# Three groups of modulation columns, not four, over the four merge rounds of a fused transformer block

## The chip, the core and the metric

The kernel runs on one core of one Trainium2 chip. The metric is device microseconds of one execution. A core has a matrix engine (PE, with its weight loads shown as PEld), a vector engine (DVE), an activation engine (ACT), a general engine (POOL) and a queue engine (SP). Each works through its own instructions in order and waits on semaphores for the others. 16 DMA engines, shared by all queues, bring data in from memory.

## What is computed

Two transformer blocks on 256 tokens of width 2048, in float32. Most of the work is products of the 256 rows with weight matrices of 2048 rows and more. The second block is modulated: shifts, scales and gates come from one small product,

```
cond = silu(c)                       # 2048 values
mod  = cond @ mod_w + mod_b          # mod_w: 2048 x 12288
sh1, sc1, g1, sh2, sc2, g2 = split(mod, 6)
```

Nothing in the first block needs `mod`. The first block is: a mixer with three branches whose gated results are merged and projected (`w_o`), a cross attention, and a feed-forward (up 2048 to 2 x 4096 in two halves, a width-3 convolution, silu gate, down 4096 to 2048). The second block begins with the normalized, modulated input of its convolution mixer.

## The kernel before

**Weights.** Every weight matrix passes through SBUF in units of 512 KB (128 x 1024 values), four slots (`SLOTS`) in rotation. SP loads a unit into `raw`; ACT writes the rounded part `w_hi` (`round_units`, L613); DVE writes the rest `w_lo` (`rest_units`, L622); PE multiplies with both. A unit's `w_hi` can be written once PE is through with the unit four before it, and a unit's `raw` slot is free once its `w_lo` is written. A chunk is 512 result columns: eight units in most stages. The argument `k` of `rest_units` counts units from the start of a chunk; its range usually runs from 4 to 12, since DVE works ahead of PE.

**Modulation.** `mod` is computed beside the first block, in 8 groups of 1536 columns. A group is 16 units, one for each 128 rows of `mod_w`: POOL loads 128 x 1536 values into one of two buffers `mod_raw` (`load_mod`, L2195), DVE multiplies by a value of `cond` and adds into `mod_acc` (`mod_unit`, L1448; the first of a group, L1445, only multiplies). POOL's load number n waits for unit n - 2. After 16 units PE transposes `mod_acc` with 12 small matmuls (`mod_sum`, L1455) and DVE reduces and stores (`mod_keep`, L1463); the next group's first unit comes after that in DVE's order. The transposes go to banks 1 to 3 of `small`.

**The order on DVE is written by hand.** `rest_units(dve, s, first, last, between, times)` spreads `times` units over `last - first` weight units: after the n-th weight unit it makes those numbered from `n * times // of` to `(n + 1) * times // of`. Behind each weight chunk DVE also has the chunk's own work. The tables say how many units of modulation go where:

- the merge has 4 rounds; in each, chunks m = 0 to 2 (gates, 8 units each) and m = 3 to 5 (branches, 4, 2 and 2 units). One group per round: 5, 5, 4, 2, 0, 0 units. At the end of m = 3, 4, 5 DVE multiplies the sums by the gates (L2718), which frees the PSUM bank for the chunk two later
- `mix_out` (4 chunks): group 4, as 5, 5, 4, 2. `cross_q`: 6 units (`MOD_CROSS`)
- the feed-forward: for each half f four up pairs i (a chunk m = 0 and a chunk m = 1), `MOD_UP[f][i]` units in each, and four down chunks c with `MOD_DOWN[f][c]`. Where (f, i) is in `MOD_KEPT`, a group is summed and stored in chunk m = 0

In an up pair PE's matmuls go four banks at once (`multiply_two`, L701 and L703). Behind each up chunk DVE adds two halves of a result (`up_sum`, L2790), waits for ACT's newest tap, and makes two rows of taps (`up_tap`, L2808) between weight units; behind the pair it makes the product, its rounded part and its rest (L2852, L2855, L2857), the last of which tells PE that `y` is ready (`ff_split`). PE needs the fourth such `y` at the seventh unit of down chunk 0.

In the second half's down chunks DVE adds the sums to `h` (L2585), ACT squares them, DVE multiplies by `norm_final` (L2891, `nf_final`), and PE waits for that before the third unit of the next chunk (`down_before`, tile 4), where it transposes `h` (L935). In `down_ffn` the chunk c = 0 starts its own `rest_units` only at k = 7 (`LATE`), so its modulation units are spread over k = 7 to 10; the other chunks spread theirs over k = 4 to 10.

Of the kernel before, what the change touches and what calls it, by code (L numbers as in the profile page):

```python
# [26 lines left out]
KT = D // P  # L27
CH = 512
UK = 2
SLOTS = 4  # L30
# [161 lines left out]
def build_program(nc, x, mem, w_in, dn_conv, dn_a_log, dn_dt_bias, dn_norm, norm_mix, swa_sinks, w_br_dn, w_br_swa,  # L192
# [68 lines left out]
    with ExitStack() as ctx:  # L261
# [848 lines left out]

        def mem_norm_pe(pe):
            yield 10
            pe.wait_ge(mod_kept, 4)
            pe.wait_ge(norm_scaled, TT)
            for g in range(NG):
                turn_rows(pe, 1, mem_x, g, g + 1)
                yield 2
# [23 lines left out]
        def cross_norm_pe(pe):  # L1141
            yield 1
            pe.wait_ge(norm_gained, 2 * NG)
            mod_sum(pe, 5 * KT)
            yield 3
            pe.wait_ge(mod_kept, 5)
            pe.wait_ge(norm_scaled, 2 * TT)
            for g in range(0, NG, 2):
                turn_rows(pe, 2, norm_x2, g, g + 2)
                yield 1  # L1150
# [11 lines left out]
        def cross_norm_dve(dve, own):  # L1162
            rms_mean_dve(dve, 2)
            yield 1
            rms_rstd_dve(dve, own, 2)
            scale_rows(dve, h, norm_x2)
            yield 1
            mod_keep(dve, own, 4, 5)
            yield 1
            for g in range(0, NG, 2):  # L1170
                split_channels(dve, own, 2, norm_v2, y_hi, y_lo, g, g + 2)
                yield 1
# [892 lines left out]
        FF_STEPS = 4 * (FF_TAPS - 1)  # L2065
        LATE = 3
        MOD_CROSS = 6
        MOD_UP = (((0, 0), (3, 2), (2, 3), (0, 4)), ((2, 2), (0, 3), (2, 2), (2, 2)))
        MOD_KEPT = ((0, 3), (1, 1))
        MOD_DOWN = ((2, 2, 2, 2), (2, 2, 1, 0))  # L2070
        MERGE_L = (32, 6)
        w_in0, up0, down0, w1, w2 = w_in[0], w_up[0], w_down[0], mlp_w1_2[0], mlp_w2_2[0]

# [500 lines left out]
        def _(dve):  # L2574
# [120 lines left out]

            def merge(i, beside):
                L = (i, *MERGE_L)
                kt = 0

                def first_chunk(j):  # L2700
                    mod_unit(dve, j, j, (i, KT))
                    if j == 1 and not isinstance(i, int):
                        split_merged(bass.ds(i * 4 - 4, 4), at(0, (i, 1)))

                for m, units in enumerate((5, 5, 4, 2, 0, 0)):
                    s = spot("merge", m, L)
                    if m == 3 and beside is not None:
                        beside.rest()
                    end = s.size + SLOTS - (1 if m >= 3 else 0)
                    rest_units(dve, s, SLOTS, end,  # L2710
                               first_chunk if m == 0 else lambda j: mod_unit(dve, kt + j, kt + j, (i, KT)), units, beside)
                    kt += units
# [15 lines left out]
                    rest_units(dve, s, end, end + 1)  # L2728

            merge(0, beside)  # L2730
# [5 lines left out]
            for c, units in enumerate((5, 5, 4, 2)):  # L2736
                s = spot("mix_out", c % 2, (c // 2, 16, 2))

                def between(j):
                    mod_unit(dve, 4 * KT + kt + j, kt + j)  # L2740
# [14 lines left out]
            rest_units(dve, s, *ahead(s), lambda j: mod_unit(dve, 5 * KT + j, j), MOD_CROSS)  # L2755
            s = spot("mem_v", 0)
            beside = Beside(cross_soft_dve(dve, own))
            rest_units(dve, s, *ahead(s), beside=beside)
# [62 lines left out]
            for f in range(2):  # L2821
# [3 lines left out]
                for i in range(4):  # L2825
                    s = spot("ffn_up", 0, L, (i, 16, 2))
                    if (f, i) in MOD_KEPT:
                        rest_units(dve, s, SLOTS + LATE, s.size + 1)
                        mod_keep(dve, own, 5 + f, 6 + f)
# [233 lines left out]
        def _(pe):  # L3063
# [58 lines left out]
            def turn_merged(i):  # L3122

                pe.wait_ge(merge_sum, i + 1)
                pe.wait_ge(mod_kept, i + 1)
                for b in range(4):
                    for t in range(TT):
                        ins = pe.transpose(small[:, b // 2, (b % 2) * T + t * P:(b % 2) * T + (t + 1) * P],
# [10 lines left out]

                return before  # L3140

            def sum_before(i):

                def before(tile, end):
                    if tile == 2:
                        if i:
                            pe.wait_ge(merged, i)
                        mod_sum(pe, at(KT, (i, KT)))

                return before  # L3150

            def merge(i, beside):
                L = (i, *MERGE_L)
                for m in range(3):
                    multiply(pe, spot("merge", m, L), x_hi, x_lo, False,
                             before=merge_before(i - 1) if i and m == 0 else None, beside=beside)
                if beside is not None:
                    beside.rest()
                for m, k0 in ((3, 0), (4, 8), (5, 12)):
                    if i == 0:  # L3160
                        pe.wait_ge(y_split, m - 1)
                    multiply(pe, spot("merge", m, L), y_hi, y_lo, False, k0=k0, before=sum_before(i) if m == 5 else None)

            merge(0, beside)
            for i in range(1, 4):
# [44 lines left out]
            def half(f, first):  # L3210
                L = (f, FFN_U, FFN_C)
                for i in range(first, 4):
                    for m in range(2):
                        s = spot("ffn_up", m, L, (i, 16, 2))
                        if m and (f, i) in MOD_KEPT:
                            pe.wait_ge(mod_kept, 6 + f)
# [128 lines left out]
```

## Time and profile before

| | |
|---|---|
| median of 3 runs | 2616.12 us (2614.69 to 2625.41) |
| profiled execution | 2616.85 us, of which the profile's span is 2614.5 us |
| PE busy | 2552.7 us (98%) |
| PE weight loads busy | 2185.4 us (84%) |
| DVE busy | 1876.8 us (72%) |
| ACT busy | 1288.3 us (49%) |
| memory traffic | 553.14 MB, mean 212 GB/s, in 40 slices between 109 and 352 GB/s |
| mean granted clock of PE | 0.995 |

The page of the profile gives busy time by engine, the span in 40 slices, the chain of work that ended last and the costliest groups of instructions. PE's busy time is modelled (matmuls overlap), so a PE busy for 98% still has to be asked how far apart its matmuls start. On the chain that ended last PE has 79%, DVE 8%, DMA 7%, and of that the load of `mod_raw` 5%. In time, the merge rounds lie at about 420 to 790 us, `mix_out` and cross attention to 998 us, the feed-forward to 1545 us.

### The profile page before, as it was taken

To read this page: it belongs to the slowest core of one execution; us is meant where nothing else is said; L and a number is where in the kernel's file an instruction comes from. 1 tells how busy PE (TensorE), PEld (TensorE's weight loads), DVE (VectorE), ACT (ScalarE), POOL (GpSimd) and SP (SyncE) were. 2 spreads that over 40 slices of the span, in tenths; PEclk is the share of its full clock that TensorE was granted. 3 is DMA by queue.
4 is the path that set the end of the run, shared out by engine and by line. 5 is a ranking of instruction groups with operands and counts; after the bars stand their busy time and mean duration, and the time that the engine had idled before them with its cause. 6 is when DMAs were issued, how large, how long until landed. Compare 5 with 4: busy or idle time off the path is not lost.

```text
span 2614.5 us, 39013 instructions
## 1 busy us (share of the span) xinstructions
PE 2552.7 (98%) x14498; PEld 2185.4 (84%) x14498; DVE 1876.8 (72%) x2098; ACT 1288.3 (49%) x1681; POOL 235.5 (9%) x270
## 2 busy tenths in 40 slices
PE   8999999999999999999999999998999999999999
PEld 7888888877887888888888879996788888888887
DVE  6796658877888768887688757988566565565564
ACT  5645445543444446554455556676544344443443
POOL 2000000010010000000000005772000000000000
PEclk9999999999999999999999999998999999999999
DMA  6643437898999765778877744543555656666655
GB/s 210 173 133 109 136 114 268 298 319 302 320 352 326 257 220 173 249 269 283 262 242 258 245 154 147 160 153 113 177 171 189 194 178 195 183 192 193 192 186 168
DMA packets 291489, 553.14 MB, mean 212 GB/s; under 512 B 17121, under 2 KB 96018, under 8 KB 290578
## 3 DMA queue, kind: packets, MB, share of 16 engines
q1 hardware_dynamic: 270994, 442.06, 52.4%
q0 software_dynamic: 18720, 102.77, 11.7%
q10 hardware_dynamic: 1632, 6.29, 0.6%
q8 instruction: 103, 1.69, 0.3%
q14 instruction: 40, 0.33, 0.0%
HBM read 548.96 MB, written 2.10 MB: 211 GB/s over the span
## 4 chain that ended last, share of the span: by engine, by line
PE 79%; DVE 8%; DMA 7%; ACT 3%; issue 3%; SPq 0%; POOLq 0%; DVEq 0%; ACTq 0%
PE sums L668 30%; PE small L668 10%; PE small L701 9%; PE sums L701 9%; PE small L703 5%; DMA mod_raw<-in_mod_w_dram 5%; PE sums L703 4%; PE sums L720 4%; DVE w_lo L622 2%; PE sums L722 2%; DVE mod_acc L1448 2%; ACT w_hi L613 1%; PE small L1811 1%; DMA raw<-in_w_br_dn_dram 1%; PE sums L1948 0%
## 5 line engine op out<-in xcount | busy, mean ns | idle before, releaser
L613 ACT ACTIVATE w_hi<-raw 128x1024 fp32r<-128x1024 f32 x814 | 859.5, 1060 | 1179.3 <-PE sums L668 364.3
L622 DVE TENSOR_TENSOR w_lo<-raw,w_hi 128x1024 fp32r<-128x1024 f32 x814 | 1003.1, 1242 | 579.5 <-ACT w_hi L613 576.9
L701 PE MATMUL sums<-x_two,w_hi 128*128 128x512 f32 x1024 | 363.3, 399 | 4.0 <-DVE x_two L1046 2.3
L701 PE MATMUL small<-x_two,w_hi 128*128 128x512 f32 x1024 | 361.2, 397 | 0.0
L703 PE MATMUL sums<-x_two,w_lo 128*128 128x256 f32 x1024 | 288.0, 281 | 0.0
L703 PE MATMUL small<-x_two,w_lo 128*128 128x256 f32 x1024 | 287.4, 281 | 0.0
L668 PE MATMUL sums<-w_hi,x_two 128*128 128x512 f32 x896 | 281.7, 392 | 0.7 <-DVE w_lo L622 0.7
L668 PE MATMUL sums<-w_hi,y_hi 128*128 128x512 f32 x672 | 265.6, 395 | 13.6 <-issue 7.2
L668 PE MATMUL sums<-w_hi,y_lo 128*128 128x512 f32 x672 | 263.1, 392 | 0.0
L668 PE MATMUL sums<-w_lo,y_hi 128*128 128x512 f32 x672 | 263.0, 391 | 0.0
L1448 DVE SCALAR_TENSOR_TENSOR mod_acc<-mod_raw,cond,mod_acc 128x1536 f32<-128x1536 f32 x120 | 217.8, 1815 | 58.2 <-DMA mod_raw<-in_mod_w_dram 58.1
L701 PEld LDWEIGHTS sums<-x_two,w_hi 128*128 128x128 f32 x1024 | 193.0, 188 | 51.5 <-issue 5.0
L701 PEld LDWEIGHTS small<-x_two,w_hi 128*128 128x128 f32 x1024 | 192.2, 188 | 46.9
L720 PE MATMUL sums<-x_two,w_hi 128*128 128x512 f32 x608 | 221.4, 406 | 2.9 <-DVE w_lo L622 1.0
L668 PEld LDWEIGHTS sums<-w_hi,x_two 128*128 128x128 f32 x896 | 168.2, 188 | 36.8 <-DVE w_lo L622 1.1
L703 PEld LDWEIGHTS sums<-x_two,w_lo 128*128 128x128 f32 x1024 | 194.2, 190 | 0.2
L703 PEld LDWEIGHTS small<-x_two,w_lo 128*128 128x128 f32 x1024 | 193.4, 189 | 0.0
L668 PE MATMUL sums<-w_lo,x_two 128*128 128x512 f32 x448 | 174.4, 389 | 0.0
L722 PE MATMUL sums<-x_two,w_lo 128*128 128x256 f32 x608 | 170.4, 280 | 0.0
L668 PEld LDWEIGHTS sums<-w_hi,y_hi 128*128 128x128 f32 x672 | 127.2, 189 | 42.9 <-issue 9.2
L2195 POOL DMA_DIRECT2D mod_raw<-in_mod_w_dram x126 | 67.1, 532 | 1025.2 <-DVE mod_acc L1448 806.4
L1991 POOL TENSOR_TENSOR cv<-cv,cv_p 128x512 f32<-128x512 f32 x96 | 151.0, 1572 | 41.6 <-ACT cv_p L1975 29.6
(432 smaller groups left out, 3950.9 us busy)
## 6 DMA issues: line engine op xcount, KB each, us to landing
raw<-in_mlp_w_dram SPq DMA_DIRECT2D x256, 512.0 KB, 4.3
raw<-in_w_in_dram SPq DMA_DIRECT2D x198, 512.0 KB, 4.6
mod_raw<-in_mod_w_dram POOLq DMA_DIRECT2D x128, 768.0 KB, 6.5
raw<-in_w_up_dram SPq DMA_DIRECT2D x128, 512.0 KB, 4.4
raw<-in_w_down_dram SPq DMA_DIRECT2D x64, 512.0 KB, 4.6
raw<-in_conv_w_in_dram SPq DMA_DIRECT2D x128, 256.0 KB, 3.8
raw<-in_w_o_dram SPq DMA_DIRECT2D x32, 512.0 KB, 6.3
raw<-in_conv_w_out_dram SPq DMA_DIRECT2D x32, 512.0 KB, 4.0
```

Of the source, the lines that this page charges most:

```text
L613: act.activation(w_hi[:, s.slot(k), :], raw[:, s.slot(k), :], ACT.Copy).then_inc(hi_ready, 1)
L622: dve.tensor_tensor(w_lo[:, s.slot(k), :], raw[:, s.slot(k), :], w_hi[:, s.slot(k), :].bitcast(F32), ALU.subtract).then_inc(lo_ready, 1)
L668: mm = pe.matmul(o, l, r, start=first and i == 0, stop=end and i + 1 == len(steps), skip_group_check=True)
L701: pe.matmul(to[:, b, :], w_hi[:, s.slot(k), c], both, start=kt == 0, stop=False, skip_group_check=True)
L703: mm = pe.matmul(to[:, b, 0:T], w_lo[:, s.slot(k), c], x_two[:, kt, 0, :], start=False, stop=kt == KT - 1, skip_group_check=True)
L720: pe.matmul(sums[:, s.pair, b, :], w_hi[:, s.slot(k), c], both, start=kt == 0, stop=False, skip_group_check=True)
L722: mm = pe.matmul(sums[:, s.pair, b, 0:T], w_lo[:, s.slot(k), c], x_two[:, kt, 0, :], start=False, stop=kt == KT - 1, skip_group_check=True)
L1448: dve.scalar_tensor_tensor(out=mod_acc[:, :], in0=mod_raw[:, m % 2, :], scalar=c, in1=mod_acc[:, :], op0=ALU.mult, op1=ALU.add).then_inc(m ...
L1811: both = [pe.matmul(small[rows_of(d), bank + d, c], lhs[rows_of(d), c], rhs[rows_of(d), c], start=m == 0, stop=True, skip_group_check=True ...
L1991: ins = pool.tensor_tensor(o, o, cv_p[:, m % PRODUCTS, :, :], ALU.add)
L2195: pool.dma_start(mod_raw[:, slot, :], src).then_inc(mod_loaded[slot], 16)
```

## The change

The merge rounds take 12 units of modulation each, 48 in all, so three groups in place of four; a group now ends in round 1 at chunk 1, in round 2 at chunk 2 and in round 3 at chunk 5. Every later group moves one place on: `mix_out` makes group 3, `cross_q` begins group 4, and the feed-forward makes 58 units in place of 42, with three groups summed in up pairs and the last in the down chunks as before. The loads of POOL follow by themselves. DVE's loop over rounds 1 to 3 is written out.

```diff
         def mem_norm_pe(pe):
             yield 10
-            pe.wait_ge(mod_kept, 4)
+            pe.wait_ge(mod_kept, 3)
...
-            mod_sum(pe, 5 * KT)
+            mod_sum(pe, 4 * KT)
             yield 3
-            pe.wait_ge(mod_kept, 5)
+            pe.wait_ge(mod_kept, 4)
...
-            mod_keep(dve, own, 4, 5)
+            mod_keep(dve, own, 3, 4)
...
         MOD_CROSS = 6
-        MOD_UP = (((0, 0), (3, 2), (2, 3), (0, 4)), ((2, 2), (0, 3), (2, 2), (2, 2)))
-        MOD_KEPT = ((0, 3), (1, 1))
-        MOD_DOWN = ((2, 2, 2, 2), (2, 2, 1, 0))
+        MOD_MERGE = ((3, 3, 3, 2, 1, 0), (4, 0, 4, 2, 1, 1), (4, 4, 0, 2, 1, 1), (3, 3, 3, 2, 1, 0))
+        MOD_ENDS = ((1, 1), (2, 2), (3, 5))
+        MOD_UP = (((0, 0), (3, 2), (2, 3), (0, 4)), ((0, 4), (3, 3), (3, 3), (0, 4)))
+        MOD_KEPT = ((0, 3), (1, 0), (1, 3))
+        MOD_DOWN = ((3, 3, 3, 3), (4, 4, 4, 0))
...
-                for m, units in enumerate((5, 5, 4, 2, 0, 0)):
+                for m, units in enumerate(MOD_MERGE[i]):
...
                     if m < 3:
+                        if (i, m) in MOD_ENDS:
+                            q = MOD_ENDS.index((i, m))
+                            mod_keep(dve, own, q, q + 1)
                         continue
...
-                        mod_keep(dve, own, i, at(1, (i, 1)))
+                        if (i, m) in MOD_ENDS:
+                            mod_keep(dve, own, 2, 3)
...
-            with own.loop(4, 2, 1) as i:
+            for i in range(1, 4):
                 merge(i, None)
...
             def mods():
-                for m in range(5 * KT + MOD_CROSS, 8 * KT):
+                for m in range(4 * KT + MOD_CROSS, 8 * KT):
...
-                pe.wait_ge(mod_kept, i + 1)
+                if i:
+                    pe.wait_ge(mod_kept, i)
...
-            def sum_before(i):
+            def sum_before(i, m):
 
                 def before(tile, end):
-                    if tile == 2:
-                        if i:
-                            pe.wait_ge(merged, i)
-                        mod_sum(pe, at(KT, (i, KT)))
+                    if tile == (2 if m == 5 else 8):
+                        pe.wait_ge(merged, i)
+                        mod_sum(pe, KT * (MOD_ENDS.index((i, m)) + 1))
...
                     if tile == 8:
-                        added(pe, spot("ffn_up", 1, (f, FFN_U, FFN_C), (i - 1, 16, 2)))
-                        mod_sum(pe, (6 + f) * KT)
+                        if i:
+                            added(pe, spot("ffn_up", 1, (f, FFN_U, FFN_C), (i - 1, 16, 2)))
+                        else:
+                            added(pe, *(spot("ffn_down", m, (f - 1, FFN_U, FFN_C), (1, 16, 2)) for m in range(2)))
+                        mod_sum(pe, (5 + MOD_KEPT.index((f, i))) * KT)
```

## Rows read from the trace of the kernel before

**Rows 1.** Page, parts 5 and 6: ACT's rounding, and the modulation's loads (KB, us to landing).

```profile
L613 ACT ACTIVATE w_hi<-raw 128x1024 fp32r<-128x1024 f32 x814 | 859.5, 1060 | 1179.3 <-PE sums L668 364.3
...
mod_raw<-in_mod_w_dram POOLq DMA_DIRECT2D x128, 768.0 KB, 6.5
```

**Rows 2.** Windows: three merge rounds, then the second half's four up pairs (the columns are named).

```profile
core 0: us, PE busy (x) PEld busy (x) DVE busy (x) ACT busy (x) POOL busy (x), PEclk, DMA share, GB/s
509.35:605.62 96.27, 91.99 (x406) 74.90 (x405) 74.29 (x57) 37.64 (x36) 8.48 (x16) 0.98 0.90 306
605.62:696.85 91.23, 89.60 (x405) 74.08 (x404) 72.37 (x56) 37.55 (x36) 8.48 (x16) 1.00 0.92 319
696.85:786.85 90.00, 89.58 (x405) 74.09 (x404) 74.08 (x57) 37.54 (x36) 8.48 (x16) 1.00 0.92 327
1268.36:1450.56 182.20, 182.20 (x1038) 158.27 (x1036) 143.60 (x155) 89.37 (x103) 7.96 (x15) 1.00 0.76 247
```

**Rows 3.** Timeline, PE, merge: start us, us, engine, line, operation [idle before, releaser].

```profile
601.26 0.80 PE L668 MATMUL sums<-w_hi,y_hi 128*128 128x512 f32 x1 [2.69 <-DVE gate L2718]
...
605.62 1.47 PE L1455 MATMUL small<-ident,mod_acc 128*128 128x128 f32 x12
...
693.99 0.50 PE L668 MATMUL sums<-w_hi,y_hi 128*128 128x512 f32 x1 [1.63 <-DVE gate L2718]
...
784.00 0.50 PE L668 MATMUL sums<-w_hi,y_hi 128*128 128x512 f32 x1 [0.42 <-DVE gate L2718]
```

**Rows 4.** Timeline, DVE: first half of the feed-forward, second up pair, three units close together.

```profile
1056.41 1.22 DVE L2852 TENSOR_TENSOR ff_v<-ff_v,ff_g 128x1024 f32<-128x1024 f32 x1
...
1059.54 2.36 DVE L622 TENSOR_TENSOR w_lo<-raw,w_hi 128x1024 fp32r<-128x1024 f32 x2
1061.81 1.81 DVE L1448 SCALAR_TENSOR_TENSOR mod_acc<-mod_raw,cond,mod_acc 128x1536 f32<-128x1536 f32 x1
...
1064.67 1.81 DVE L1448 SCALAR_TENSOR_TENSOR mod_acc<-mod_raw,cond,mod_acc 128x1536 f32<-128x1536 f32 x1
...
1071.95 1.82 DVE L1448 SCALAR_TENSOR_TENSOR mod_acc<-mod_raw,cond,mod_acc 128x1536 f32<-128x1536 f32 x1 [4.33 <-DMA mod_raw<-in_mod_w_dram]
...
1074.82 1.22 DVE L2790 TENSOR_TENSOR pad<-sums,pad 128x1024 f32<-128x1024 f32 x1
...
1078.01 1.68 DVE L2808 SCALAR_TENSOR_TENSOR ff_g<-pad,par,ff_g 128x256 f32<-128x256 f32 x4 [0.83 <-ACT ff_g L2424]
```

**Rows 5.** Timeline, POOL: the load issued after the unit that starts at 1061.81.

```profile
1064.35 0.53 POOL L2195 DMA_DIRECT2D mod_raw<-in_mod_w_dram  x1 [114.30 <-DVE mod_acc L1448]
```

**Rows 6.** Timeline, DVE: third up pair, first and last of three units.

```profile
1125.26 1.81 DVE L1448 SCALAR_TENSOR_TENSOR mod_acc<-mod_raw,cond,mod_acc 128x1536 f32<-128x1536 f32 x1
...
1135.59 1.82 DVE L1448 SCALAR_TENSOR_TENSOR mod_acc<-mod_raw,cond,mod_acc 128x1536 f32<-128x1536 f32 x1 [1.84 <-DMA mod_raw<-in_mod_w_dram]
```

**Rows 7.** Timeline, PE: the starts of the two down-projections, and a wait in the first.

```profile
1180.24 0.40 PE L668 MATMUL sums<-w_hi,y_hi 128*128 128x512 f32 x1
...
1197.50 0.50 PE L668 MATMUL sums<-w_hi,y_hi 128*128 128x512 f32 x1 [0.77 <-DVE y_lo L2857]
...
1450.56 0.40 PE L668 MATMUL sums<-w_hi,y_hi 128*128 128x512 f32 x1
```

**Rows 8.** Timeline, DVE: around the first chunk of the second down-projection.

```profile
1463.68 1.23 DVE L2857 TENSOR_TENSOR y_lo<-ff_v,y_hi 128x1024 fp32r<-128x1024 f32 x1
...
1473.83 1.22 DVE L2585 TENSOR_TENSOR h<-sums,h 128x1024 f32<-128x1024 f32 x1
...
1477.08 1.29 DVE L2891 TENSOR_TENSOR h<-h,final_b 128x512 f32<-128x512 f32 x2 [0.90 <-ACT nf_sq L899]
```

**Rows 9.** Timeline, PE: the wait in that projection's second chunk, and a long one later.

```profile
1478.43 1.09 PE L935 MATMUL small<-ident,h 128*128 128x128 f32 x8 [0.50 <-DVE h L2891]
...
1796.92 0.77 PE L668 MATMUL sums<-w_hi,y_hi 128*128 128x512 f32 x1 [7.18 <-issue]
```

**Rows 10.** The tile mod_raw, 1045 to 1545 us: its loads, issue to landing.

```profile
DMA to landing us min/median/max: 4.4/6.1/8.5
```

More of the change, by code:

```diff
@@ L2697, in merge, with next_merge @@
                 L = (i, *MERGE_L)
-                kt = 0
+                def next_merge(j):
+                    n = next(merge_mods)
+                    mod_unit(dve, n, n % KT)
                 def first_chunk(j):
-                    mod_unit(dve, j, j, (i, KT))
-                    if j == 1 and not isinstance(i, int):
-                        split_merged(bass.ds(i * 4 - 4, 4), at(0, (i, 1)))
-                for m, units in enumerate((5, 5, 4, 2, 0, 0)):
+                    next_merge(j)
+                    if j == 1 and i:
+                        split_merged(slice(i * 4 - 4, i * 4), i)
+                for m, units in enumerate(MOD_MERGE[i]):
                     s = spot("merge", m, L)
@@ L2709, in merge @@
                     end = s.size + SLOTS - (1 if m >= 3 else 0)
-                    rest_units(dve, s, SLOTS, end,
-                               first_chunk if m == 0 else lambda j: mod_unit(dve, kt + j, kt + j, (i, KT)), units, beside)
-                    kt += units
+                    rest_units(dve, s, SLOTS, end, first_chunk if m == 0 else next_merge, units, beside)
                     if m < 3:
+                        if (i, m) in MOD_ENDS:
+                            q = MOD_ENDS.index((i, m))
+                            mod_keep(dve, own, q, q + 1)
                         continue
@@ L2726, in merge @@
                                           ALU.add).then_inc(merge_sum, 1)
-                        mod_keep(dve, own, i, at(1, (i, 1)))
+                        if (i, m) in MOD_ENDS:
+                            mod_keep(dve, own, 2, 3)
                     rest_units(dve, s, end, end + 1)
+            merge_mods = iter(range(3 * KT))
             merge(0, beside)
-            with own.loop(4, 2, 1) as i:
+            for i in range(1, 4):
                 merge(i, None)
@@ L2739, in between @@
                 def between(j):
-                    mod_unit(dve, 4 * KT + kt + j, kt + j)
+                    mod_unit(dve, 3 * KT + kt + j, kt + j)
                     if c == 0 and j == 1:
@@ L2754, in _ @@
             s = spot("cross_q", 0)
-            rest_units(dve, s, *ahead(s), lambda j: mod_unit(dve, 5 * KT + j, j), MOD_CROSS)
+            rest_units(dve, s, *ahead(s), lambda j: mod_unit(dve, 4 * KT + j, j), MOD_CROSS)
             s = spot("mem_v", 0)
@@ L2828, in _ @@
                         rest_units(dve, s, SLOTS + LATE, s.size + 1)
-                        mod_keep(dve, own, 5 + f, 6 + f)
+                        q = 4 + MOD_KEPT.index((f, i))
+                        mod_keep(dve, own, q, q + 1)
                         rest_units(dve, s, s.size + 1, s.size + SLOTS)
@@ L3140, in merge_before @@
                 return before
-            def sum_before(i):
+            def sum_before(i, m):
                 def before(tile, end):
-                    if tile == 2:
-                        if i:
-                            pe.wait_ge(merged, i)
-                        mod_sum(pe, at(KT, (i, KT)))
-                return before
+                    if tile == (2 if m == 5 else 8):
+                        pe.wait_ge(merged, i)
+                        mod_sum(pe, KT * (MOD_ENDS.index((i, m)) + 1))
+                return before if (i, m) in MOD_ENDS else None
             def merge(i, beside):
@@ L3155, in merge @@
                     multiply(pe, spot("merge", m, L), x_hi, x_lo, False,
-                             before=merge_before(i - 1) if i and m == 0 else None, beside=beside)
+                             before=merge_before(i - 1) if i and m == 0 else sum_before(i, m), beside=beside)
                 if beside is not None:
@@ L3161, in merge @@
                         pe.wait_ge(y_split, m - 1)
-                    multiply(pe, spot("merge", m, L), y_hi, y_lo, False, k0=k0, before=sum_before(i) if m == 5 else None)
+                    multiply(pe, spot("merge", m, L), y_hi, y_lo, False, k0=k0, before=sum_before(i, m))
             merge(0, beside)
@@ L3215, in half @@
                         if m and (f, i) in MOD_KEPT:
-                            pe.wait_ge(mod_kept, 6 + f)
+                            pe.wait_ge(mod_kept, 5 + MOD_KEPT.index((f, i)))
                         multiply_two(pe, s, m, sum_up(f, i) if m == 0 and (f, i) in MOD_KEPT else None)
```

## The prediction, made before the changed kernel was run

> **What bounds the kernel now.** I read the page first: PE is busy 98% of the span, so time can only come from the few places where PE waits, and can go wherever the change makes it wait. Then I followed the chain of waits in order of time. In the merge rounds it runs again and again through a modulation unit and the load of `mod_raw`; in the feed-forward it is almost only PE. The windows by round say how much that is: the three whole rounds last 96.27, 91.23 and 90.00 us with the same matmuls, while the DMA engines are 90 to 92% busy at 306 to 327 GB/s [rows 2]. PE's timeline shows where: before the last branch chunk PE waits 2.69, 1.63 and 0.42 us for the gate product on DVE [rows 3], which stands behind a modulation unit that waited for its load. Five units in 8 weight units (21.8 us) want a load every 4.4 us; with two buffers a load of 6.5 us [rows 1] plus the unit and POOL's issue gives one every 4.8 us. So the merge is bound by the modulation's loads, the feed-forward by PE, and DVE has room there: 143.60 us busy in 182.20 [rows 2]. The question is whether the 16 units that move there fit between two weight units, not on average.
>
> **Prices of DVE's steps, from one burst.** Start to start, two w_lo take 2.27 us (1.14 each) before a unit that starts at 1061.81; the next unit starts 2.86 later, so a unit takes 1.73 [rows 4]. The three instructions from L2852 take 3.13 us, an L2790 1.13, four taps 1.6, and the wait for ACT's tap before them 0.83 [rows 4]. An up pair of DVE is 16 w_lo (18.2) + 2 L2790 (2.3) + four rows of taps (6.4) + 3.1 + two waits (1.7) = 31.7 us. PE needs 45.2 us for the pair: four pairs and one sum (1.3) are 182.20 us [rows 2, 3]. A w_lo can start when PE is through with the unit four before it and ACT has made its w_hi (1.06 us [rows 1], 1.3 with the signals): (k - 3) units and 1.3 us into a chunk, a unit being 2.83 us in an up chunk and 2.73 in a down chunk (ten of them in the 27.37 us from 1450.56 to PE's idle 0.50 before 1478.43 [rows 7, 9]).
>
> **The price of three units in a row.** Both buffers are full at the first two, but the third unit's load is issued only after the first unit: at 1064.35, 2.54 us after that one's start [rows 5]. The third starts 10.14 us after the first, with DVE idle for 4.33 us, in front of every later w_lo [rows 4]. In chunk m = 1, where the three are spread over k = 7, 9, 10, first to third is 10.33 us [rows 6]; the work between is 6.9 us, so 3.5 us idle if DVE is behind anyway (1.84 where it was not).
>
> **Part 1, merge: 16 units fewer.** A clean round is 90.00 less the third round's wait of 0.42 and the 0.3 of its restart, 89.3 us. Excess: 7.0 + 1.9 + 0.7 = 9.6 us [rows 2, 3]; the first includes PE at half clock after the wait (0.98 of 96.27 us [rows 2], 1.7 us). With 12 units the round moves 16.8 + 9.4 = 26.2 MB, 293 GB/s at 89.3 us, under the 327 that the third round reached [rows 2]. Chunks with 4 units want a load every 5.45 us, more than 4.8. What hides the rest: each gate product has 5.4 us (the two units of the chunk between), in which a unit of 1.73 us, now also in m = 4 and m = 5 of rounds 1 and 2, has room beside two w_lo and the product. I take 9.0 us gained; between 7 and 9.6, as one wait of about 2 us may stay. The moved `mod_sum` and `mod_keep` cost nothing net: 8 groups before and after; where they stand in chunk 1 or 2, PE asks for the last unit at its fifth weight unit, 10.9 us into the chunk, and DVE has it at 1.3 + 1.14 + 1.73, about 4. The unrolled loop is at nothing, no wait of DVE being put down to its loop; 0 to 0.5.
>
> **Part 2, mix_out and cross attention:** the same numbers of units at the same places, one group earlier. Nothing.
>
> **Part 3, first down-projection, c = 0 (2 to 3 units, at k = 8, 9, 10).** DVE's y is ready 17.1 us after the chunk's start: PE waited 0.77 us for it until 1197.50, and 1180.24 is the start [rows 7]. Then w_lo twice (19.4), the burst (third unit at up to 29.5, until 31.3), the add and w_lo of unit 11: 33.5. PE wants that at 17.3 + 5 x 2.73 = 30.9. With the burst of rows 4 this costs 2.6 us; with a median landing of 6.1 [rows 10] 1.1. I take 1.5 (0 to 2.7).
>
> **Part 4, second half, up pairs.** Pair 0 gets the sum and (0, 4), which is just what pair 3 of the first half has today: it ends with y at 17.1 in the next chunk, 2.8 us later than after a pair of (2, 2) (14.3, part 5), and costs PE nothing by itself. Pairs 1 and 2 get (3, 3): 31.7 + 6 x 1.73 + 4.33 + 3.5 = 49.9 us on DVE against 45.2 on PE. The bursts exist in the first half too, as (3, 2) and (2, 3), where 31.7 + 8.7 + 4.3 = 44.7 just fits. So each of the two pairs is 4.7 us too long. DVE's lead of some two units takes 1.5 of it, as y at 17.1 is that far ahead of where w_lo of k = 7 would be late (8th unit, 19.8 us, less 1.14). 9.4 - 1.5 = 8 us. Ends: if loads land in 6.1 rather than 7.6 us, each of the four stalls shrinks by 1.5, and 2 x 1.7 - 1.5 = 2 us stay; the upper end is the whole 9.5.
>
> **Part 5, second half, last pair and down chunk c = 0.** The pair now holds (0, 4): y at 17.1 instead of 14.3 (1463.68 + 1.2 less 1450.56) [rows 7, 8]. PE needs it at 16.3: 0.9 us. Then four units at k = 7 to 10, one behind each w_lo: `eff` 0.3, w_lo, first unit at 18.5, third at 18.5 + 10.1 = 28.7, w_lo of k = 10 until 31.5, fourth at 32.5 (its load issued 2.5 us after the second's start at 21.4, and landing in up to 8.5 [rows 10]), the add at 34.2. Today the add starts at 1473.83, and PE's transposes come 4.6 us later, at 1478.43, 27.9 us after the chunk's start [rows 8, 9]. After: 34.2 + 4.6 = 38.8. **+11 us**, the largest term; behind the late add stand ACT's squares, L2891, PE's transposes and all its later matmuls. With landings at 6.1 it is 8.5; with y at 18.6, 13.
>
> PE is then idle for some 10 us at one place. Today's row with 7.18 us of idle [rows 9] and the first of rows 3 are followed by matmuls at 1.2 GHz in place of 2.4. Rows 2 price the smaller at 1.7 us; I take **2** (0 to 2.7).
>
> **Part 6, down chunks 1 and 2: 4 units each, at k = 5, 7, 9, 10.** The last two are adjacent, and the load of the last is issued after the unit at k = 7: the unit at k = 7 ends at 4 x 2.73 + 1.3 + 1.14 + 1.73 = 15.1 us in the chunk, its load is there 8.3 later (0.8 to the issue, 7.5 to landing), at 23.4, the unit ends at 25.1 and the add starts, against 23.3 today in c = 0 (1473.83 less 1450.56 [rows 7, 8]). 1.8 us each at most, to PE one for one, since it waits there today already (0.50 [rows 9]). **+3** (0.5 to 4.5).
>
> **Sum.** -9.0 + 1.5 + 8 + 11 + 2 + 3 = +16.5 us. On the span of 2614.5: 2631.0; 2.35 us lie around it (2616.85), and the median is 0.7 under the profiled execution: **2632.6 us**. All ends together: +1.4 to +25.4, 2617.5 to 2641.5.
>
> The Trainium skill, "SBUF — State Buffer", section "The DMA setup-cost knee", speaks against this sum: a load costs about 2 us plus its bytes at 436 GB/s, 3.8 us for 768 KB by its figure (an estimate), and with that the burst would stall DVE by 0.6 us and the feed-forward would lose little. The trace differs, with 6.5 us in the median [rows 1], as loads share the engines with the weights; its nearest row is the shortest landing, which is the next rival's.
>
> **Rivals.**
> - *Loads land fast.* While DVE stands still no `raw` slot comes free, so weight loads pause and `mod_raw` has the engines alone: 4.4 us is the shortest landing [rows 10]. A third unit then starts 7.0 us after the first: 1.3 us idle. Pairs: 43.5 us, no loss. Part 5: y 17.1 or less, add at 29 to 30, +5.5. Parts 3 and 6: 1 together; clock 1. -9 + 5.5 + 2 = -1.5: **2614.6** (2609 to 2619). For it: landings of 4.4 to 5 where one load is alone. Against: the burst itself, 7.6 us, after DVE had stood still.
> - *The room is there* (the other side). DVE has 38.6 us idle in 182.20 [rows 2]; the waits move into it and only the merge shows: -8 to -10, **2607**. It decides in c = 0 of the second half: if the third unit starts by 24 us, the add is before 28 and PE waits no longer than today. Against: two buffers; the wait cannot be shorter than a landing.
> - *The merge keeps its waits*, because weights and not the modulation fill the 16 engines: DVE still waits in the 4-unit chunks. Gain 3 instead of 9, and the bursts at their upper ends, +8: **2645**. Against: 327 GB/s reached, 293 wanted.
>
> **Chances.** Forecast (2617.5 to 2641.5) 0.62, of it 0.14 below 2629; loads land fast 0.17; room 0.12, of it 0.04 below 2603; merge keeps its waits 0.09. About 0.5% (13 us) is what a measurement tells from no change. Faster 0.04, same 0.14 + 0.17 + 0.08 = 0.39, slower 0.48 + 0.09 = 0.57. Range 2610 to 2641: it takes in most of the fast loads and leaves out 0.10 on either side.
>
> **What would show it.** Windows of rounds 1 to 3 of 89 to 90 us and DMA at about 295 GB/s (part 1). In DVE's timeline: idle of 3 to 4.5 us before the third of each burst; L2585 of c = 0 at 34 us after the start of the second down-projection, and before PE's first L935 there about 9 us idle, followed by some us at 1.2 GHz. Up pairs 1 and 2 of the second half at 49 to 50 us in place of 45.2, the first less DVE's lead. If the pairs stay at 45.2, part 4 is wrong; if that L935 is less than 3 us late, part 5 is, and the time falls to 2615 or below.

## The result, and the profile after

The change costs 0.29% (ratio to the kernel before 1.0029, 95% interval 1.0019 to 1.0039): 2625.67 us, the median of 20 runs, against 2618.46 us for the kernel before, also 20 runs. One of after's twenty ran at a lower granted clock (3591 us) and is left out of ratio and ranges. That is +7 us where +16.5 was forecast. The loss is clear of zero, but it is under the 0.5% that the forecast called no change, and the time lies in the part of the forecast range (below 2629 us) that was given a chance of only 0.14. The forecast time of 2632.6 us is off by 7 and not by 9 only because its base, the median of three runs, was 2.3 us too low.

The profiled execution of after took 2635.2 us, 2632.7 of them its span, so +18.2 us against the profiled execution of before. It lies at the upper end of after's runs (2618.57 to 2635.2), while the profiled one of before is a little under its median. The profile tells where time went; how much, the medians and the experiments tell.

Windows of after: the three whole merge rounds and the second half's four up pairs, as in [rows 2].

```profile
core 0: us, PE busy (x) PEld busy (x) DVE busy (x) ACT busy (x) POOL busy (x), PEclk, DMA share, GB/s
512.89:602.18 89.29, 89.29 (x405) 74.18 (x404) 64.58 (x52) 37.64 (x36) 5.81 (x11) 1.00 0.86 283
602.18:692.25 90.07, 89.52 (x405) 74.10 (x404) 67.92 (x54) 37.66 (x36) 6.33 (x12) 1.00 0.87 296
692.25:781.55 89.30, 89.30 (x406) 74.16 (x404) 68.27 (x52) 37.66 (x36) 6.86 (x13) 1.00 0.90 306
1263.44:1453.03 189.59, 184.71 (x1049) 159.16 (x1048) 149.20 (x160) 88.80 (x103) 10.04 (x19) 1.00 0.78 259
```

PE is busy for all of two rounds. The three last 268.66 us, against 277.50 in [rows 2]: 8.8 gained. The up pairs last 189.59 in place of 182.20 us. Of these 7.4, 4.9 are idle time of PE, which had none there, 1.3 are the sum that moved in, and 1.2 are longer busy time of the other matmuls.

The same view by smaller stretches: first down-projection, chunks 0 and 1; second down-projection, chunks 0 and 1, then 2 and 3 with what follows, up to the convolution mixer.

```profile
1170.94:1219.92 48.98, 45.74 (x194) 37.03 (x193) 39.40 (x38) 19.39 (x21) 3.69 (x7) 0.97 0.81 278
...
1453.03:1509.66 56.63, 49.15 (x203) 40.02 (x201) 45.50 (x43) 23.39 (x33) 4.63 (x9) 0.91 0.81 274
1509.66:1567.15 57.49, 51.47 (x239) 41.70 (x238) 36.42 (x41) 30.19 (x55) 2.23 (x5) 0.97 0.62 208
```

For these, windows of before.

```profile
1180.24:1224.84 44.60, 43.83 (x195) 35.98 (x194) 36.25 (x36) 19.39 (x21) 2.65 (x5) 1.00 0.84 290
1450.56:1495.73 45.17, 44.67 (x203) 36.80 (x201) 35.69 (x38) 23.51 (x33) 2.12 (x4) 1.00 0.77 264
```

Span less busy time is PE's idle time, and busy time grows where the clock is halved. In the second projection's chunks 0 and 1, idle grows from 0.50 to 7.48 us, busy from 44.67 to 49.15 at a granted clock of 0.91: 7.0 + 4.5 = 11.5 us. In the first projection it is 2.5 + 1.9 = 4.4 us. From its start to the convolution mixer the feed-forward takes 1567.15 - 989.16 = 578.0 us in after and 1550.79 - 998.50 = 552.3 in before: +25.7, of which 1.3 are the moved sum.

DVE's timeline of after, chunk 0 of the first down-projection, which starts at 1170.94: first and third unit.

```profile
1190.10 1.81 DVE L1448 SCALAR_TENSOR_TENSOR mod_acc<-mod_raw,cond,mod_acc 128x1536 f32<-128x1536 f32 x1
...
1200.42 1.82 DVE L1448 SCALAR_TENSOR_TENSOR mod_acc<-mod_raw,cond,mod_acc 128x1536 f32<-128x1536 f32 x1 [4.51 <-DMA mod_raw<-in_mod_w_dram]
```

DVE's timeline of after, chunk 0 of the second down-projection, which starts at 1453.03 (answers [rows 8]).

```profile
1470.85 1.23 DVE L2866 TENSOR_TENSOR y_lo<-ff_v,y_hi 128x1024 fp32r<-128x1024 f32 x1
...
1473.42 1.81 DVE L1448 SCALAR_TENSOR_TENSOR mod_acc<-mod_raw,cond,mod_acc 128x1536 f32<-128x1536 f32 x1
1475.15 1.22 DVE L622 TENSOR_TENSOR w_lo<-raw,w_hi 128x1024 fp32r<-128x1024 f32 x1
1476.29 1.81 DVE L1448 SCALAR_TENSOR_TENSOR mod_acc<-mod_raw,cond,mod_acc 128x1536 f32<-128x1536 f32 x1
1478.01 1.22 DVE L622 TENSOR_TENSOR w_lo<-raw,w_hi 128x1024 fp32r<-128x1024 f32 x1
1480.90 1.82 DVE L1448 SCALAR_TENSOR_TENSOR mod_acc<-mod_raw,cond,mod_acc 128x1536 f32<-128x1536 f32 x1 [1.67 <-DMA mod_raw<-in_mod_w_dram]
1482.64 1.22 DVE L622 TENSOR_TENSOR w_lo<-raw,w_hi 128x1024 fp32r<-128x1024 f32 x1
1484.22 1.82 DVE L1448 SCALAR_TENSOR_TENSOR mod_acc<-mod_raw,cond,mod_acc 128x1536 f32<-128x1536 f32 x1 [0.36 <-DMA mod_raw<-in_mod_w_dram]
1485.96 1.22 DVE L2587 TENSOR_TENSOR h<-sums,h 128x1024 f32<-128x1024 f32 x1
```

PE's timeline of after: its waits in the second down-projection (answers [rows 9]).

```profile
1472.13 0.80 PE L668 MATMUL sums<-w_hi,y_hi 128*128 128x512 f32 x1 [2.59 <-DVE y_lo L2866]
...
1489.57 1.97 PE L935 MATMUL small<-ident,h 128*128 128x128 f32 x8 [4.89 <-DVE h L2900]
...
1516.14 1.10 PE L935 MATMUL small<-ident,h 128*128 128x128 f32 x8 [0.88 <-DVE h L2900]
...
1540.68 1.09 PE L935 MATMUL small<-ident,h 128*128 128x128 f32 x8 [1.64 <-DVE h L2900]
```

The mechanism is the forecast's: `y` late, the burst, the late add, the late transposes. But there are two long waits, not one: first for `y`, 19.1 us into the chunk, then for `h`, at 36.5 us.

### The profile page after: what moved, and what is told of

Its sections match the earlier page's. It is cut to its first block, busy times and chain, and to the rows that moved or that the text cites. A ratio compares the mean times of both kernels' runs of the same rounds, so it can differ in the third digit from the quotient of the medians.

```text
span 2632.7 us, 38871 instructions
## 1 busy us (share of the span) xinstructions
PE 2558.5 (97%) x14498; PEld 2189.6 (83%) x14498; DVE 1875.9 (71%) x2098; ACT 1287.7 (49%) x1681; POOL 234.9 (9%) x270
## 3 DMA queue, kind: packets, MB, share of 16 engines
q8 instruction: 103, 1.69, 0.3%
## 4 chain that ended last, share of the span: by engine, by line
PE 80%; DVE 10%; DMA 4%; ACT 3%; issue 2%; POOL 0%; SPq 0%; POOLq 0%; ACTq 0%; DVEq 0%
PE sums L668 36%; PE small L668 9%; PE small L701 7%; PE sums L701 7%; PE sums L720 4%; PE small L703 4%; PE sums L703 4%; DMA mod_raw<-in_mod_w_dram 3%; DVE w_lo L622 3%; DVE mod_acc L1448 2%; PE sums L722 2%; ACT w_hi L613 1%; PE small L1811 1%; DVE ff_v L2816 1%; PE sums L1948 0%
```

## The experiments

Each is compared with the kernel before in interleaved runs on the same chip. There were three occasions, and before had medians of 2617.97, 2618.62 and 2618.79 us. The second (`half_load`, `up_even`, `down_two`, `rebal2`) was on another chip than the first and third, so differences between occasions go by the ratios. Edits are against the changed kernel.

**The change once more**, unedited.

> The changed kernel itself, once more, since its profiled execution was 18 us over the one of before while the medians of twenty lay 7 us apart. Theory A (the waits come from loads of the modulation that two buffers cannot hide, and a load's landing time differs from execution to execution): +7 us in the median (2 to 12), and a profile in which the same places wait, each by another amount: the down chunk after the second half's last pair 3 to 10 us, the up pairs with (3, 3) 0 to 4 us each. Theory B (the profiled execution was disturbed as a whole): a profile at +7 with the first merge rounds and everything else in the same proportion.

2626.74 us, ratio 1.0037 (1.0022 to 1.0053). Its profiled span is 2625.4 us; the feed-forward takes 578.2 us again, yet up to the feed-forward it is 5.6 us faster than the first profile of after. So 5.6 of the 7.3 us between these two spans lie before the feed-forward; the loss inside it repeats.

**The merge part alone.**

```diff
-        MOD_UP = (..., ((0, 4), (3, 3), (3, 3), (0, 4)))
-        MOD_KEPT = ((0, 3), (1, 0), (1, 3))
-        MOD_DOWN = ((3, 3, 3, 3), (4, 4, 4, 0))
+        MOD_UP = (..., ((2, 2), (0, 3), (2, 2), (2, 2)))
+        MOD_KEPT = ((0, 3), (1, 1))
+        MOD_DOWN = ((2, 2, 2, 2), (2, 2, 1, 0))
...
-                for m in range(4 * KT + MOD_CROSS, 8 * KT):
+                for m in range(4 * KT + MOD_CROSS, 7 * KT):
```

> Twelve units a merge round as in the change, but the eighth group of modulation columns is left out (its loads, units and sum; its values are zero), so that the feed-forward has the 42 units of the kernel before at the same places. It shows the gain of the merge alone. Theory A: -9 us against before (-7 to -10.5). Rival (the merge's waits are mostly the weights' own, part of the gain is not real in most executions): -3 us.

2605.45 us, ratio 0.9954 (0.9938 to 0.9970): -12.5 us. One sum (1.3 us of PE) went with the omitted group, so the merge part is worth 11.2 us, more than the 7 to 10.5 that were expected. Its feed-forward, which has the units of before, takes 554.0 us in the profile.

**The feed-forward part alone.**

```diff
-        MOD_MERGE = ((3, 3, 3, 2, 1, 0), (4, 0, 4, 2, 1, 1), (4, 4, 0, 2, 1, 1), (3, 3, 3, 2, 1, 0))
-        MOD_ENDS = ((1, 1), (2, 2), (3, 5))
+        MOD_MERGE = ((5, 5, 4, 2, 0, 0),) * 4
+        MOD_ENDS = ((0, 5), (1, 5), (2, 5), (3, 5))
...
-                for m in range(4 * KT + MOD_CROSS, 8 * KT):
+                for m in range(5 * KT + MOD_CROSS, 9 * KT):
```

> The merge with 16 units a round as before, and the feed-forward with the 58 units of the change, the sixteen more being the last group a second time (ninth group, the same columns read and stored again). It shows the cost of the feed-forward alone. Theory A: +16 us in the median (the change's +7 and the 9 that the merge gives), up to +25 in the profiled execution. Rival (the cost is a small one in most executions, 2 or 3 us, and the merge gives nothing): +5 to +8.

2634.79 us over six runs, ratio 1.0068 (1.0044 to 1.0092): +17.8 us by the ratio (11.5 to 24), 16.5 without the sum of the added group. The other way round, the whole change less the merge part alone is 2626.74 - 2605.45 = 21.3 us on the same occasion, 20.0 without that sum. So the feed-forward part costs 16 to 20 us, the merge part gives 11, and between them they leave +5 to +9: the measured +7 to +10 needs nothing else.

PE's timeline of this kernel, whose merge is that of before, also corrects the first term. Before the last branch chunks of rounds 2 and 3:

```profile
691.61 0.79 PE L668 MATMUL sums<-w_hi,y_hi 128*128 128x512 f32 x1 [3.56 <-DVE gate L2728]
...
786.40 0.50 PE L668 MATMUL sums<-w_hi,y_hi 128*128 128x512 f32 x1 [3.79 <-DVE gate L2728]
```

In [rows 3] the same places show 1.63 and 0.42 us. In round 1 it is the other way round, 1.54 us here and 2.69 in before. The three rounds together take 280.94 us here (509.90 to 790.84), 277.50 in before: the profiled execution of before had got off lightly, by some 3 us.

**Half the bytes of each late load.** All instructions stay, and landings get shorter. The kernel leaves out half of the columns of groups 5 to 7, so it also moves fewer bytes in all.

```diff
-            load_groups(1, 6)
+            load_groups(1, 5)
+            load_groups(5, 6, MOD_W // 2)
...
-            load_groups(6, MOD_G)
+            load_groups(6, MOD_G, MOD_W // 2)
```

> The change with all its units at their places, but each load from group 5 on brings only the left half of the columns (384 KB in place of 768); the units compute on what is in the buffer, so that three groups are not the reference's. It shows whether the landing time sets the cost. Theory A: landings of 4 to 5 us, idle before a third unit of 0 to 1 us in place of 3 to 5, pairs 1 and 2 at 45.2 to 46 us, the wait before L935 at 2 to 4 us in place of 5 to 7.6: 12 to 16 us off the change, about -5 us against before. Rival (DVE's instructions themselves are too many for these places): the waits stay and the time at +5 to +9.

2615.58 us, ratio 0.9995 (0.9985 to 1.0005): 9 to 11 us of the feed-forward's loss are gone (12 to 16 were expected) with DVE's work unchanged. The median landing from 1045 to 1545 us falls from 6.1 to 4.6 us. Its window of the second half's up pairs shows no idle time of PE at all:

```profile
1256.31:1439.82 183.51, 183.51 (x1050) 159.56 (x1048) 152.13 (x161) 89.03 (x103) 10.70 (x20) 1.00 0.72 227
```

So the loss in the up pairs is waiting for loads, not DVE's arithmetic. Chunk 0 of the second projection, which starts at 1439.82, keeps an idle 4.86 us before L935, and the second down-projection still takes 108.1 us (100.2 in before). Here DVE hardly waits for loads any more. Its timeline:

```profile
1464.49 1.82 DVE L1448 SCALAR_TENSOR_TENSOR mod_acc<-mod_raw,cond,mod_acc 128x1536 f32<-128x1536 f32 x1 [0.38 <-DMA mod_raw<-in_mod_w_dram]
...
1467.70 1.82 DVE L1448 SCALAR_TENSOR_TENSOR mod_acc<-mod_raw,cond,mod_acc 128x1536 f32<-128x1536 f32 x1 [0.25 <-DMA mod_raw<-in_mod_w_dram]
1469.43 1.22 DVE L2588 TENSOR_TENSOR h<-sums,h 128x1024 f32<-128x1024 f32 x1
```

The add starts 29.6 us into the chunk, against 23.3 in before. That is `y` at 17.1 in place of 14.3, and two units more of 1.73 us each. In after the add came at 32.9. So of its 9.6 us of lateness there, 6.3 are DVE's own instructions and their order, and 3.3 go with the loads.

**Pairs 1 and 2 without the (3, 3)**, their two units placed in pair 0, in an interval that was empty.

```diff
-        MOD_UP = (..., ((0, 4), (3, 3), (3, 3), (0, 4)))
+        MOD_UP = (..., ((2, 4), (2, 3), (2, 3), (0, 4)))
...
-                        rest_units(dve, s, s.size + 1, s.size + SLOTS)
+                        rest_units(dve, s, s.size + 1, s.size + SLOTS - 1, next_mod, MOD_UP[f][i][0])
+                        rest_units(dve, s, s.size + SLOTS - 1, s.size + SLOTS)
```

> The change, with the six units of pairs (3, 3) taken apart: pair 0 of the second half takes two more behind its store, pairs 1 and 2 have (2, 3). All other places are the change's. Theory A (a pair with six units has two loads too late and is longer than PE's): windows of pairs 1 and 2 back at 45.2 us from 47 to 49, 4 to 7 us off the change's time, so about +3 us against before. Rival (DVE's lateness comes in from pair 0's (0, 4) and stays): pairs 1 and 2 stay over 46 us and the time at +7 to +9.

2621.87 us, ratio 1.0016 (1.0005 to 1.0027): some 4 us back, as expected. Both pairs last 45.2 us again; the second down-projection keeps its loss (1560.97 - 1446.87 = 114.1 us).

**Two units out of chunk 0, into pair 3** in front of it (the second edit above is in it too).

```diff
-        MOD_UP = (..., ((0, 4), (3, 3), (3, 3), (0, 4)))
+        MOD_UP = (..., ((0, 4), (3, 3), (3, 3), (2, 4)))
...
-        MOD_DOWN = ((3, 3, 3, 3), (4, 4, 4, 0))
+        MOD_DOWN = ((3, 3, 3, 3), (2, 4, 4, 0))
```

> The change, with two of the four units of the second half's down chunk 0 moved into the first chunk of the pair before, behind the store. Theory A (the late add of chunk 0 is what PE waits for, 5 to 7.6 us before its first L935, and half clock after it): that wait back under 1 us, of the 8 to 10 us one or two come back at y, since pair 3 now has six units: 6 to 8 us off the change, about +1 us against before (-1 to +4). Rival (the two units cost the same in pair 3, as DVE is late there in any case): +6 to +9, with the wait at y instead.

2622.02 us, ratio 1.0016 (1.0004 to 1.0029): 3 to 5 us back where 6 to 8 were expected. The wait for `h` is gone, but the fuller pair makes `w_lo` and `y` late (PE idle 1.77 and 2.78 us), and the second down-projection still takes 108.2 us, against 100.2 in before.

**Two units out of chunk 0, into chunk 3**, where DVE makes them behind its first two weight units.

```diff
-        MOD_DOWN = ((3, 3, 3, 3), (4, 4, 4, 0))
+        MOD_DOWN = ((3, 3, 3, 3), (2, 4, 4, 2))
...
-                        rest_units(dve, s, SLOTS, end - 2)
+                        rest_units(dve, s, SLOTS, SLOTS + 2, next_mod, MOD_DOWN[f][c])
+                        rest_units(dve, s, SLOTS + 2, end - 2)
```

> The changed kernel, but the first chunk of the second down-projection has 2 modulation units again in place of 4 and the last chunk has the other 2, behind its first two weight units (both loads have landed by then). Isolates part 5's largest term, the burst in chunk c = 0. Theory: with two units no load is waited for; from y (19.0 us into the chunk in the changed kernel's profile) DVE needs 0.3 + 4 w_lo (4.6) + 2 units (3.5), so the add starts at 27.4 and PE's transposes L935 come at 32.0 us instead of 36.5; the second down-projection falls from 114 to 109 to 110 us, and the median by 3 to 5 us against the change (ratio to before 1.001, between 1.000 and 1.002). The wait for y (2.6 to 2.8 us) stays, as pairs 1 to 3 still have ten units. Rival: y's lateness is what is paid, and the transposes' wait would only move behind it or into chunks 1 and 2 (4 units each, unchanged): second down-projection 112 us or more, gain under 1.5 us.

2618.62 us, ratio 1.0003 (0.9986 to 1.0021): 7 to 9 us back, more than the expected 3 to 5, from moving two units. The second down-projection takes 105.6 us, where 109 to 110 were expected. The add is early, the transposes come 32.0 us into the chunk, as expected, and the half clock that followed them is gone too (1.00 in the 4 us from 1476.78, 0.50 in after). PE's timeline:

```profile
1463.50 0.75 PE L668 MATMUL sums<-w_hi,y_hi 128*128 128x512 f32 x1 [2.25 <-DVE y_lo L2866]
...
1476.78 1.09 PE L935 MATMUL small<-ident,h 128*128 128x128 f32 x8 [0.50 <-DVE h L2901]
```

This kernel's up pairs are instruction for instruction those of the change, and they show what a burst costs when its third load lands early. DVE's timeline of it, pair 1:

```profile
1324.68 1.81 DVE L1448 SCALAR_TENSOR_TENSOR mod_acc<-mod_raw,cond,mod_acc 128x1536 f32<-128x1536 f32 x1
1327.54 1.81 DVE L1448 SCALAR_TENSOR_TENSOR mod_acc<-mod_raw,cond,mod_acc 128x1536 f32<-128x1536 f32 x1
1332.34 1.82 DVE L1448 SCALAR_TENSOR_TENSOR mod_acc<-mod_raw,cond,mod_acc 128x1536 f32<-128x1536 f32 x1 [1.85 <-DMA mod_raw<-in_mod_w_dram]
```

And of after, the same three units:

```profile
1329.94 1.81 DVE L1448 SCALAR_TENSOR_TENSOR mod_acc<-mod_raw,cond,mod_acc 128x1536 f32<-128x1536 f32 x1
1332.80 1.81 DVE L1448 SCALAR_TENSOR_TENSOR mod_acc<-mod_raw,cond,mod_acc 128x1536 f32<-128x1536 f32 x1
1339.90 1.82 DVE L1448 SCALAR_TENSOR_TENSOR mod_acc<-mod_raw,cond,mod_acc 128x1536 f32<-128x1536 f32 x1 [4.14 <-DMA mod_raw<-in_mod_w_dram]
```

First to third is 7.66 us in one and 9.96 in the other; the loads were issued 2.53 and 2.54 us after the first unit and landed after 5.1 and 7.4 us. Pair 1 then lasts 45.2 us (nothing lost) and 47.5 us.

**No burst that needs a third load, wherever that could be had** (units in the kept pair's chunk m = 0 placed as in the second edit of the pairs experiment).

```diff
-        MOD_UP = (((0, 0), (3, 2), (2, 3), (0, 4)), ((0, 4), (3, 3), (3, 3), (0, 4)))
-        MOD_DOWN = ((3, 3, 3, 3), (4, 4, 4, 0))
+        MOD_UP = (((0, 0), (3, 2), (2, 3), (1, 4)), ((2, 4), (2, 3), (2, 3), (2, 4)))
+        MOD_DOWN = ((2, 3, 3, 3), (2, 4, 4, 0))
```

> The change's merge and the same 58 units in the feed-forward, placed otherwise: one or two units of each summed pair stand in its first chunk behind the store, so that no pair has (3, 3) and the first down chunk of either half has two units instead of three and four. Theory A (only where units stand closer than a load can land do they cost): the merge's gain stays, and of the cost only the two chunks with four units and the 0.9 us at y: -5 us against before (-3 to -8). Rival (the sixteen units cost DVE or the DMA engines time wherever they stand): +5 to +8, as the change.

2612.19 us, ratio 0.9982 (0.9967 to 0.9997), as expected. Then the four-unit chunk m = 1 of pair 3 thinned in both halves as well, with the edit of chunk 3:

```diff
+        MOD_UP = (((0, 0), (3, 2), (2, 3), (2, 2)), ((2, 4), (2, 3), (2, 3), (2, 2)))
+        MOD_DOWN = ((2, 3, 3, 4), (2, 4, 4, 2))
```

> As rebal, with pairs 3 of both halves at two and two units, the rest in down chunks where there is room: four in the first half's last, and two at the start of the second half's last chunk, ahead of PE's sum. Theory A: y in time at both down-projections (waits of 1.5 and 2.8 us in rebal gone), else as rebal: -8 us against before (-6 to -11), 3 to 4 us under rebal. Rival (the units in the second half's last chunk delay the last sum or the last adds): not under rebal, -5 or above.

2609.67 us, ratio 0.9970 (0.9959 to 0.9982).

> The same kernel as rebal2 (units moved so that no burst of three needs a third load in the second half's pairs 0 and 3 nor in down chunk 0), once more, to see whether the gain against the kernel before repeats on another occasion. Theory: ratio 0.997 again (0.996 to 0.998), 2610 us, second down-projection 102 to 104 us, up pairs of the second half without idle time of PE. Rival: the gain came from landing times of one occasion: ratio 0.999 or more.

2609.42 us, ratio 0.9963 (0.9950 to 0.9975). This version beats both kernels: 8 to 10 us under before, 16 or more under the change, with the same units, groups and loads. Of the 11.2 us of the merge part it keeps all but 1.5 to 3. Its windows (the four up pairs; second down-projection, chunks 0 and 1):

```profile
1253.17:1436.67 183.50, 183.50 (x1050) 159.54 (x1048) 153.13 (x162) 89.61 (x103) 10.73 (x21) 1.00 0.82 278
1436.67:1481.84 45.17, 44.67 (x203) 36.79 (x201) 38.90 (x39) 23.42 (x33) 3.06 (x6) 1.00 0.81 278
```

DVE does 4 us more here than in after's up pairs (153.13 against 149.20), in 6 us less time, and PE never waits. Nor do the loads land sooner: their median from 1045 to 1545 us is 6.9 us here and 6.1 in after. What fell is DVE's waiting for them, from 35.3 us in 17 waits to 15.2 in 9. So it is the places of the units that count, and DVE's busy share said nothing about the loss. What is left are the transposes before chunks 2 and 3 (idle 1.26 and 1.09 us), behind chunks with four units.

A third buffer for `mod_raw` should take away the wait for a third load too. It wasn't tried, and no run shows whether there is room for it.

## Why the prediction was right in its direction and too large

The direction and the main cause were right: the room on DVE is average room, and two buffers can't serve three units in a row without a wait. The size was not, and the small errors of several terms partly cancel. Term by term, by the prediction's parts:

- **Part 1, merge, -9.0: too small a gain.** The forecast of 89.3 us for a clean round is what two rounds show; at 283 to 306 GB/s the DMA engines keep up, so the rival in which the merge keeps its waits is out. But the 9.6 us of excess came from one execution with mild waits; by the medians it is about 11.2. What failed is taking [rows 3] as typical. Starts of the feed-forward agree: 998.5 and 1000.3 us in the two profiles with the merge of before, 983.6 to 991.5, in the mean 987.5, in the ten with the new one. A load every 4.8 us was also too slow: [rows 5] and a landing of 6.5 give 2.54 + 6.5 = 9.0 us for two loads, 4.5 each, still over the 4.4 wanted.
- **Part 2, nothing.** Within what executions differ by; no run isolates it.
- **Part 3, first down-projection, +1.5: measured +4.4** in the profile (2.5 idle, 1.9 half clock). The arithmetic of the burst held: first unit 19.2 us into the chunk (forecast 19.4), third at 29.5 (forecast, the upper end: 29.5). The step that failed is the choice of a middle value where this execution had one of the longest bursts, and it left out the clock. In the six profiles with the same units there, this down-projection takes 90.1 to 92.5 us, against 88.1 and 88.9 with the units of before, so the usual cost is nearer 3.
- **Part 4, up pairs, +8: measured +6.1** in the profile (7.4 less the sum), and 4 in the medians for pairs 1 and 2. DVE stalls 2.05 to 4.25 us before the third units of these pairs, 4.33 and 3.5 assumed; pairs 1 and 2 last 47.5 and 48.6 us, where 49 to 50 were named. With landings of 4.7 to 8.2 us in the same code this term was 1.7 us in one profile (185.24 - 182.20 - 1.3) and 6.1 in another. DVE also waited in pair 3 (2.82 and 1.51 us), which had been left at nothing, so `y` came at 19.1, not 17.1. The late pair 2 in front is the smaller part of this: in `up_even`, with pairs 1 and 2 in time, DVE waited 2.38 and 1.38 us there and `y` still came at 18.4.
- **Part 5, chunk 0, +11 and +2: measured 7.0 idle and 4.5 half clock.** The sum of 13 is 1.5 too large, but its two terms are off in opposite ways. The add came at 32.9 (forecast 34.2), since the third and fourth loads landed in 4.9 and 5.4 us: on these two landings the rival with fast loads was right, as it was on the add at 29 to 30 with loads that land early (29.6 in `half_load`). From add to transposes it was 3.6 us, not 4.6. The half clock was priced once; there were two waits over 2 us, and each was followed by it. This part repeats best: the second down-projection takes 113.3 to 114.1 us in the four profiles that have the change's units there.
- **Part 6, chunks 1 and 2, +3: measured +1.5** (idle 0.88 and 1.64 us, 0.50 each in before). Its upper end of 4.5 was more than its own two times 1.8. The stretch as a whole grew by 2.4 (57.49 against 1550.79 - 1495.73 = 55.06). The other 0.9 is half clock behind the last transposes: L922 to the convolution mixer takes 3.20 us in after and 2.29 in before. It isn't the change's, as it takes 3.21 in `merge_only` too.

In the two profiles the feed-forward's terms add up to 24.4 and 24.6 us without the moved sum, against the 25.5 of the forecast; taken against the 554.0 us of `merge_only` in place of the 552.3 of before they are 22.7 and 22.9. In the medians it is 16 to 20. So the forecast of that stage was nearly right for the executions that were profiled and 5 to 9 us too large for the usual one; with a merge term 2 us too small, this is about the whole gap between +16.5 and +7 to +10. Why the profiles pay more than the medians isn't settled. They aren't all slow executions: the second profile of the change (2627.1 us) is at the median of its runs, with 578.2 us in its feed-forward and the earliest start of it of all twelve profiles. Pair 1, with 7.4 us and 5.1 us landings in equal code, shows that landings alone can make such a difference, not that they do.

The Trainium skill, "SBUF — State Buffer", section "The DMA setup-cost knee", gave an estimate of 3.8 us for such a load by its figure. No landing from 1045 to 1545 us was that short: after's shortest was 4.5 and its median 6.1 us. Only the halved loads (384 KB) reached 3.3, with a median of 4.6. While the bursts' loads of after were under way the DMA engines were 88% busy or more, so sharing is the likely reason; no run tests it.

## What to carry to other kernels

With two buffers here, and so by the same reasoning with n, the use after the last full buffer waits for issue plus landing however idle the engine is on average: write the uses down by position and give each stretch no more than its buffers hold, and only then look at the busy share. Then add up the engine's own instructions ahead of each result that another engine waits for, since these were late in one chunk even with quick loads. Moving work out of a bound stage can be worth nearly all of its gain, but the destination table deserves as much care as the source; here the gain of 11 us turned into a loss of 7 through where 16 units were put, and back into a gain of 9 through where they were put instead. Read a wait's size from several executions, or say that it comes from one.

## What the runs showed of the hardware

Waits of similar length differ in what follows them. Windows of after, each 4 us from the end of a wait of PE: two in up pairs (1.69 and 2.70 us), the one in the first down-projection (2.70), then `y` (2.59) and `h` (4.89).

```profile
1342.90:1346.90 4.00, 4.00 (x23) 3.52 (x24) 3.17 (x5) 2.77 (x6) 0.07 (x1) 1.00 0.80 254
1391.49:1395.49 4.00, 4.00 (x23) 3.54 (x24) 3.17 (x5) 2.77 (x6) 0.07 (x1) 1.00 0.79 248
1204.56:1208.56 4.00, 4.00 (x11) 3.20 (x12) 4.00 (x4) 0.71 (x1) 0.00 (x0) 0.61 0.87 288
1472.13:1476.13 4.00, 4.00 (x12) 3.23 (x13) 3.97 (x5) 0.00 (x0) 0.17 (x1) 0.63 0.33 84
1489.57:1493.57 4.00, 4.00 (x14) 3.52 (x15) 3.39 (x3) 3.10 (x9) 0.00 (x0) 0.50 0.84 292
```

The granted clock, the third figure from the right, falls to 0.50 to 0.63 (1.2 GHz for most of the 4 us) after three of them: 11 and 12 matmuls start after the first two, where 18 do after such a wait that was spared (1201.46 us in the second profile of the change). After the wait of 2.70 us in an up pair it stays at 1.00. In the down-projections and the merge, over the twelve profiles, waits of 2.69 us or more were followed by the lower level, none of 1.87 us or less was, and in between it went either way: after 1.90 (`ffn_only`), 2.25 and 2.59 us yes, after 2.48 us (for `y`, in the second profile of the change) and 2.64 us (for `y`, in `rebal`) no. One such wait cost 1.9 us on top of itself (45.74 - 43.83), two cost 4.5. Behind the second down-projection two waits of 1.53 and 1.55 us, 3 us apart, were followed by 0.59 in after and by 1.00 in before. In an up pair of `ffn_only` a wait of 2.87 us was followed by the lower level:

```profile
1401.86:1405.86 4.00, 4.00 (x12) 3.42 (x13) 3.17 (x5) 2.77 (x6) 0.06 (x1) 0.50 0.78 253
```

So the length of the wait alone doesn't decide it between 1.9 and 2.7 us, and what else does stays open.
